# Keys and queries of the second linear attention computed with the tokens stationary, and turned by VectorE

## The reference, cut to what matters

```python
h = rms_norm_2(x, norm_mix_pre)
z = h @ w_in                                   # p, q, k, v, g_lr, r, gate_logits = split(z)
log_a = log_sigmoid(g_lr @ w_gate_up + b_gate) / 16
# 4 heads, keys of 256, values of 512, chunks of 64 tokens; per head:
qc = q * (256 ** -0.5); G = cumsum(log_a)      # within a chunk
A[i, j] = sum_c q[i, c] * k[j, c] * exp(G[i, c] - G[j, c])    # j <= i
o = A @ v + (q * exp(G)) @ S                   # S: state carried between chunks
```

## Time and profile before

| | |
|---|---|
| median of three runs | 2775.2 us (2774.86 to 2776.15) |
| the profiled execution | 2776.08 us |
| its span, first to last instruction | 2774.3 us |
| mean granted TensorE clock | 0.999 of full |
| PE busy | 2751.3 us (99%) |
| DVE busy | 1778.4 us (64%) |
| ACT busy | 1354.2 us (49%) |
| POOL busy | 64.8 us (2%) |
| share of PE in the chain that ended last | 96% |

### The profile page before, as it was taken

The page is one execution under the profiler, slowest core; times in us unless marked ns, Lnnn a source line. Parts: engine busy times, 40 slices in busy tenths (PEclk is TensorE's granted clock), DMA queues, the critical chain, the costliest instruction groups (busy, mean ns, idle before and its releaser), DMA issues.

```text
span 2774.3 us, 36245 instructions
## 1 busy us (share of the span) xinstructions
PE 2751.3 (99%) x14792; PEld 2302.3 (83%) x14792; DVE 1778.4 (64%) x2183; ACT 1354.2 (49%) x1635; POOL 64.8 (2%) x55
## 2 busy tenths in 40 slices
PE   9999999999999999999999999999999999999998
PEld 7888888878888888888888887888878888888887
DVE  6778865576556655766778744566566546656575
ACT  5666554654444434445546545554454444444443
POOL 0000000000000000000011000000000000000000
PEclk9999999999999999999999999999999999999999
DMA  8555455556656565555555554555555555565655
GB/s 325 188 167 171 157 186 167 185 180 205 195 191 190 198 196 192 194 187 176 192 171 171 176 194 163 179 201 195 196 190 183 204 194 191 191 198 188 198 190 159
DMA packets 144424, 525.16 MB, mean 189 GB/s; under 512 B 16081, under 2 KB 16641, under 8 KB 143617
## 3 DMA queue, kind: packets, MB, share of 16 engines
q1 hardware_dynamic: 142528, 514.71, 56.3%
q0 software_dynamic: 1440, 7.88, 0.8%
q10 hardware_dynamic: 288, 0.24, 0.0%
HBM read 520.66 MB, written 2.11 MB: 188 GB/s over the span
## 4 chain that ended last, share of the span: by engine, by line
PE 96%; DVE 2%; ACT 1%; issue 1%; DMA 0%; POOL 0%; DVEq 0%; SPq 0%; POOLq 0%; ACTq 0%
PE PS L539 96%; PE PS L542 0%; DVE X L1553 0%; DVE AR L1547 0%; DVE RL L1547 0%; DVE A_HL L1553 0%; ACT RH L1051 0%; DMA RAW<-in_stream 0%; DVE B_HL L1553 0%; ACT SP L1051 0%; POOL ST L2224 0%; ACT A_HL L1051 0%; ACT B_HL L1051 0%; DVE AR L1755 0%; DVE AR L1550 0%
## 5 line engine op out<-in xcount | busy, mean ns | idle before, releaser
L1547 DVE TENSOR_TENSOR RL<-RAW,RH 128x1024 fp32r<-128x1024 f32 x954 | 1159.3, 1225 | 863.2 <-ACT RH L1051 861.8
L1051 ACT ACTIVATE RH<-RAW 128x1024 fp32r<-128x1024 f32 (+1 forms) x962 | 1014.2, 1059 | 1049.2 <-PE PS L539 1032.9
L539 PE MATMUL PS<-RH,A_HL 128*128 128x512 f32 x3520 | 1094.5, 390 | 1.4 <-DVE A_HL L1553 0.9
L539 PEld LDWEIGHTS PS<-RH,A_HL 128*128 128x128 f32 x3520 | 660.7, 188 | 139.7 <-DVE A_HL L1553 1.1
L539 PE MATMUL PS<-RH,B_HL 128*128 128x512 f32 x2240 | 692.1, 389 | 2.1 <-DVE B_HL L1553 0.9
L539 PE MATMUL PS<-RL,A_HL 128*128 128x512 f32 x1760 | 684.8, 389 | 0.0
L539 PEld LDWEIGHTS PS<-RH,B_HL 128*128 128x128 f32 x2240 | 420.4, 188 | 90.5 <-DVE B_HL L1553 1.2
L539 PE MATMUL PS<-RL,B_HL 128*128 128x512 f32 x1120 | 435.7, 389 | 0.0
L539 PEld LDWEIGHTS PS<-RL,A_HL 128*128 128x128 f32 x1760 | 330.5, 188 | 68.7 <-issue 0.7
L539 PE MATMUL PS<-A_HL,RH 128*128 128x512 f32 (+1 forms) x1488 | 360.7, 394 | 4.2 <-DVE A_HL L1553 4.2
L539 PEld LDWEIGHTS PS<-A_HL,RH 128*128 128x128 f32 (+1 forms) x1488 | 271.1, 189 | 59.1 <-issue 3.5
(11 more groups left out here) (114 smaller groups left out, 961.4 us busy)
## 6 DMA issues: line engine op xcount, KB each, us to landing
RAW<-in_stream SPq DMA_DIRECT2D x959, 512.0 KB, 4.2
X<-in_x SPq DMA_DIRECT2D x4, 512.0 KB, 7.4
AR<-in_mem SPq DMA_DIRECT2D x4, 512.0 KB, 5.8
AR<-in_mem_turned SPq DMA_DIRECT2D x4, 512.0 KB, 5.6
out_x<-X SPq DMA_DIRECT2D x8, 256.0 KB, 2.8
AR<-in_x_turned SPq DMA_DIRECT2D x3, 512.0 KB, 8.2
AR<-scratch POOLq DMA_DIRECT2D x1, 1024.0 KB, 10.1
AR<-in_mix_post_g POOLq DMA_DIRECT2D x1, 1024.0 KB, 9.0
```

The source lines that it names most:

```text
L539: return g.matmul(o, l, r, start=start, stop=stop, skip_group_check=True)
L1051: return g.activation(o, i, f, bias=bias, scale=scale, accum_out=accum)
L1547: return g.tensor_tensor(o, a, b, f)
```

## The change

The four products K0, K1, Q0 and Q1 go from `by_feature` to `by_token`, and the stream holds their weights in blocks of 512 columns (as many slots as before). ACT alone evicts them, two activations of 128x512 for each, which scale by the token's row scale (for Q by a column `query_col`, row scale times 1/16, that ACT makes in `row_task`). DVE's additions and multiplications by RR fall away for them. They land in U(7) (two places, `KQ_ROWS`, used in turn), and a new task turns them to their old homes: 16 stream transposes of 32 partitions x 256 elements for each of the four, 64 in all, spread over the ticks last(name) + 0.5 to last(name) + 2. Both halves of the levels start 2.5 slots later, DECAY + 19.5 and DECAY + 27.5, and wait for the turned keys and queries (`s_kqt`).

```diff
-    by_columns("K0", "w_in_2", 16, 2048, 2)
+    by_tokens("K0", "w_in_2", 0, 16, 2048, 2)
     passes.append(("LR", "w_in_2", 0, 16, 5120, 16, 2))
-    by_columns("K1", "w_in_2", 16, 2048 + 512, 2)
+    by_tokens("K1", "w_in_2", 0, 16, 2048 + 512, 2)
     for j in range(2):
-        by_columns(f"Q{j}", "w_in_2", 16, 1024 + 512 * j, 2)
+        by_tokens(f"Q{j}", "w_in_2", 0, 16, 1024 + 512 * j, 2)
...
-            plan, at, done = level_plan([0, 1, 2, 4, 8, 16, 32, 64, 128], DECAY + (17, 25)[j], 8, 4, 1, hg_done[j], gla_at)
+            plan, at, done = level_plan([0, 1, 2, 4, 8, 16, 32, 64, 128], DECAY + (19.5, 27.5)[j], 8, 4, 1, hg_done[j], gla_at)
...
+        KQ_HOME = [U(1)[:, 0:1024], U(1)[:, 1024:2048], U(0)[:, 0:1024], U(0)[:, 1024:2048]]
+        KQ_ROWS = [U(7)[:, 1024 * k:1024 * k + 1024] for k in range(2)]
...
                         g.wait_ge(s_z_a, 8)
-                        g.wait_ge(s_free_v, read_v[f"Q{j}"])
+                        g.wait_ge(s_kqt, 3 + j)
...
-            by_feature("K0", A_HL, normed(3))
+            by_token("K0", AH, AL, normed(3))
...
-            for n in ("K1", "Q0", "Q1", "P0", "P1", "G00", "G01", "G02", "G03"):
+            for n in ("K1", "Q0", "Q1"):
+                by_token(n, AH, AL)
+            for n in ("P0", "P1", "G00", "G01", "G02", "G03"):
                 by_feature(n, A_HL)
...
+                if n == 3:
+                    act(query_col, row_col[n], scale=0.0625).then_inc(s_rw, 1)
...
+            def keyed(n):
+                def evict(banks):
+                    g.wait_ge(s_rrs, 4)
+                    if n > 1:
+                        g.wait_ge(s_kqt, n - 1)
+                    for b in range(2):
+                        t = act(KQ_ROWS[n % 2][:, 512 * b:512 * b + 512], PS[:, banks[b], :],
+                                scale=(row_col[3], query_col)[n // 2][:, b:b + 1])
+                    t.then_inc(s_free_a, 1)
+                return evict
...
+            def keys_turn_task():
+                for n, name in enumerate(KQ):
+                    src = KQ_ROWS[n % 2].rearrange("p (b c d i) -> p b c d i", b=2, c=4, d=4)
+                    dst = KQ_HOME[n].rearrange("p (c b d i) -> p b c d i", c=4, b=2, d=4)
+                    for fq in range(4):
+                        yield last(name) + 0.5 + 0.5 * fq
+                        g.wait_ge(s_free_a, read_a[name])
+                        for tq in range(4):
+                            t = g.transpose(dst[32 * fq:32 * fq + 32, :, :, tq, :], src[32 * tq:32 * tq + 32, :, :, fq, :])
+                    t.then_inc(s_kqt, 1)
...
             def gla_inputs(j):
-                return [(s_z_v, 11 + 3 * j), (s_free_v, read_v[f"Q{j}"])]
+                return [(s_z_v, 11 + 3 * j), (s_kqt, 3 + j)]
...
-            through("K0", rowed(U(1)[:, 0:1024], 3))
+            through("K0")
...
-            through("K1", rowed(U(1)[:, 1024:2048], 3))
+            through("K1")
             for j in range(2):
-                through(f"Q{j}", rowed(U(0)[:, 1024 * j:1024 * j + 1024], 3, 0.0625))
+                through(f"Q{j}")
```

More of the change, by code:

```diff
@@ L318, in build @@
         s_vh, s_va = sem("first_values_multiplied"), sem("first_values_copied")
+        s_kqt = sem("second_keys_turned")
         s_c_m, s_c_a, s_c_v = sem("cross_by_tensor"), sem("cross_by_scalar"), sem("cross_by_vector")
@@ L343, in build @@
         ffn_readers("F")
-        by_vector += ["K0", "LR", "K1", "Q0", "Q1", "P0", "P1"] + [f"{n}{j}" for n in ("G0", "ya") for j in range(4)]
+        by_scalar += ["K0", "K1", "Q0", "Q1"]
+        by_vector += ["LR", "P0", "P1"] + [f"{n}{j}" for n in ("G0", "ya") for j in range(4)]
         by_scalar += [f"{n}{j}" for n in "VR" for j in range(4)]
@@ L406, in build @@
         GLA_END = last("V0")
+        KQ = ["K0", "K1", "Q0", "Q1"]
         def hg_at(t):
@@ L511, in build @@
         row_col = [stat(f"row_scale{n}", 2) for n in range(5)]
+        query_col = stat("query_scale", 2)
         neglam, lb, oml, subg = stat("neglam", 1), stat("lb", 8), stat("oml", 8), stat("subg", 1)
@@ L707, in row_task @@
                 g.wait_ge(s_nlo, 8 * n + 8)
-                g.wait_ge(s_rw, SPREAD[n])
+                g.wait_ge(s_rw, SPREAD[n] + (n == 3))
                 w = SP4[:, 0:T].rearrange("p (b n) -> p b n", b=2)
@@ L1474, in scalar @@
             norm(3, AH, last("Fo2_3") + 1)
-            through("K0", None, U(1)[:, 0:1024])
+            def keyed(n):
[8 more added lines that the diff above has]
+                return evict
+            through("K0", keyed(0))
             def low_rank(banks):
@@ L1480, in scalar @@
             through("LR", low_rank)
-            through("K1", None, U(1)[:, 1024:2048])
+            through("K1", keyed(1))
             for j in range(2):
-                through(f"Q{j}", None, U(0)[:, 1024 * j:1024 * j + 1024])
+                through(f"Q{j}", keyed(2 + j))
             for j in range(2):
@@ L1980, in vector @@
                           *[level_task(j, gla_plan[j], gla_homes(j), 2, [6 + j], gla_inputs(j), 2) for j in range(2)],
-                          pool_task(), gla_out_task(), row_task(4), hidden_task(0), hidden_task(1))
+                          keys_turn_task(), pool_task(), gla_out_task(), row_task(4), hidden_task(0), hidden_task(1))
             def post_part(n, b, ssq):
```

## The result

The changed kernel takes **2788.1 us** (median of 4 runs, 2787.57 to 2789.92), the kernel before 2775.4 (4 runs, 2774.86 to 2776.15): 1.0045 times as long, 95% interval 1.0033 to 1.0057. The forecast was 2776.6, which is 11.5 us less, and its range ended at 2779.5.

A forecast was written before the change was run, and what follows sets the result against it. The prediction took TensorE's pace to bound the kernel (busy 99% of the span). Pace -1.5, entry into K0 +1.4 and the wait behind Q0 +1.5 summed to +1.4 us, from 2775.2 to 2776.6 us, range 2774.0 to 2779.5.

The forecast's parts named there:

- The levels' move: Levels 2.5 slots later, takes now between two evictions: longest stretch without a low half shorter; cost 0, bounds 0 and 1.2.
- The burst behind K1: VectorE's transposes begin 3.5 us after K1's end (F); slot 462's low half in time by 0.4 us, cost nothing.
- The burst behind Q0: VectorE's transposes end 13.8 us after Q0's end (E); TensorE waits 1.5 us at level 0 in slot 469.
- The entry into K0: K0 ends at 1316.9 in place of 1315.5, its third slot waiting for a low half: cost 1.4 us, bounds 0.7 and 2.0.
- the forecast wait for the third slot: In K0, TensorE reaches the third slot at about 1298.8 and waits for VectorE's low half, starting at 1300.2.
- The pace: Slots by token take 2.721 us, by feature 2.784; 24 slots of K1, Q0 and Q1 gain 1.5 us, bounds 0 and 2.0.
- The single-matmul rule: N/2.4 + 2.5 ns per matmul: a token slot 2.590 us, a feature slot 2.600, gain 0.24 us for 24 slots.
- The chances: Whole kernel: 0.02 for faster by over 0.2%, 0.91 for within 0.2%, 0.07 for slower by over 0.2%.
- rival (d): VectorE's queue so full that each of four bursts makes a low half 1.2 us late: 2781.5 us, chance 0.07.
- the signs that were to show the forecast wrong: TensorE idle behind K0, K1 or Q1 bursts, slot pace not 2.72, or K0 ending under 0.7 or over 2 us later.
- those that were to show it right: Among them: K0's third-slot wait, a 1.5 us wait in Q1, no TensorE idle P0 to V0, VectorE over 90% busy LR to P0.

The follow-up runs named there:

- e1: Kernel before with only the two level plans moved to DECAY+19.5 and DECAY+27.5, no transposes: 2783.3 us, ratio 1.0027.
- e2: Changed kernel with the levels another 1.5 slots later, at DECAY+21 and DECAY+29: 2781.4 us, ratio 1.0019.
- e5: Changed kernel with one take and its spans, of both halves, moved from between slots 502 and 503 to behind slot 504: 2782.3 us, ratio 1.0022.
- e3: Changed kernel with the first of the decay's two exponentials on ScalarE 1.5 slots later, DECAY+8.5 instead of DECAY+7: 2784.8 us, ratio 1.0031.
- second profile: Changed kernel unchanged, profiled again in the second set of runs: span 2786.1 us; that set's median 2787.5 us, ratio 1.0041.
- e7: Changed kernel with e3's edit, levels at +21 and +29, slot 488's take at 489.5, high part first in all but each product's last slot: 2775.5 us, ratio 0.9999.
- e10: Changed kernel with e9's levels, e3's edit, and high part first in all slots of K0, K1, Q0, Q1 but each one's last: 2776.6 us, ratio 1.0003.
- e4: Changed kernel with K0's first three slots multiplying the high part first, waiting for the low part only in between: 2785.6 us, ratio 1.0035.
- e6: Changed kernel with the levels back at DECAY+17 and DECAY+25, so the transposes' part alone: 2797.0 us, ratio 1.0077.
- e9: Changed kernel with levels back at +17 and +25, except each half's first: products at DECAY+21 and +29, take and spans at +21.5 and +29.5: 2780.8 us, ratio 1.0016.

## Why the prediction was wrong

- **The levels' move, costed at 0 with bounds 0 and 1.2: this step failed, by 7.4 us** (e1). It reasoned that takes between two evictions make the longest stretch without a low half shorter, and looked for their effect on low halves and on V0's eviction. The low halves were fine. Who waited was ScalarE, for an eviction behind the takes, and then the pool through ScalarE. I had listed VectorE's fullest place (1430 to 1475) and not the stage behind it. There VectorE and ScalarE have idle time (9.4 and 15.0 of the 45 us from 1475 to 1520 in the kernel before), but the chain of dependences goes through three engines. e2, with the levels later still, shows that lateness as such does not cost this, and e5 that the place of the takes at one tick does. No rival had this mechanism.
- **The burst behind K1, costed at 0: wrong by 1.9 us of wait.** With what follows the wait, Q0 lost 2.2 us in the first profile and 3.9 in the second, where the clock fell (+1.73 and +3.35, and 0.5 of gained pace on top). The time from the burst's begin to its end was right: 1352.32 to 1360.76 are 8.4 us, and the low half of slot 462 ended 9.7 us behind the begin, as worked out. The begin was not: F + 6.0 (F = 1346.35) in place of F + 3.5. The model is from a place without decay activations, and ScalarE was passed with "idle half of the time". A share over the kernel says nothing of the two instructions that stand at one tick (e3). The margin was 0.4 us, so any such row decided.
- **The burst behind Q0, +1.5: right in the first profile** (1.54 us of idle time before level 0, its transposes over at E + 13.8 as worked out, E = 1370.36). There TensorE and VectorE both came over 2 us late out of the burst behind K1, which the working did not have. But e3, whose burst behind K1 begins at F + 3.6 as forecast, has 1.41, so this is not luck. The second profile has 0.58 there, since TensorE came about 1 us later, behind a longer Q0. Waits in a row are not independent: what is lost at one is partly given back at the next.
- **The entry into K0, +1.4: right**, +1.3 to +1.7 in the seven traces with the order of the changed kernel. The first profile hid the forecast wait for the third slot: the first slot ran in part at the lower clock (0.92 in the mean from 1295 to 1320) and took 4.7 us. e3 and e5 show the wait itself, 1.15 and 1.19 us, and the same end.
- **The pace, -1.5: right.** K1 takes 23.22 us in place of 23.71, -0.49, in all ten traces with K1 by token, and where no wait disturbs (e7, e10) K1, Q0 and Q1 gain 1.5 together. The single-matmul rule of the Trainium skill ("TensorE: Matmul & The Clock Gate", Back-to-back issue gap) would leave an estimated 0.24 us of the 1.5. The traces do not agree with it: K1 alone gains 0.49.
- **The chances.** 0.91 for within 0.2% and 0.07 for slower rested on rival (d), a full VectorE at four bursts, and it wasn't the cause: the largest loss needs no transpose (e1), one burst of four made a low half late, and that one through ScalarE (e3). The bounds "0 to 1.2" for each unknown edit were bounds for one low half, not for an instruction that others wait for.

Of the signs that were to show the forecast wrong, one came, idle time behind the K1 burst. Of those that were to show it right, two did not come besides the hidden wait in K0: TensorE had idle time between P0 and V0, and VectorE was busy for 59.4 of 69 us from LR on (86%) and not for over 90%.

By term for the second profile: entry +1.3 (forecast +1.4), pace -1.5 in K1 to Q1 (-1.5), slot 462 with the clock behind it +3.9 (0), level 0 +0.7 (+1.5), pool +6.1 (0), slots 525 and 473 to 504 +1.1 (0). Sum +11.6.

## What to carry to other kernels

An edit that only moves ticks has to be costed at every tick on which it lands: for each, list what stands behind the moved instruction in its engine's order, and who waits for those, to the second and third engine, also far behind the code that was edited. Where a burst has under 1 us of margin, read the rows of all engines at that very tick, since an idle share over the kernel hides a table load and an exponential. When a late operand meets an engine with independent work in the same slot, the order within the slot can cover it: in e4 it took K0 with its entry from +1.3 us to -0.3.

## What the runs showed of the hardware

The same idle time of TensorE was sometimes followed by a lower granted clock and sometimes not. Busy time in the 10 us around the wait at slot 462, for the first profile (us; PE, PEld, DVE, ACT and POOL busy; granted clock, DMA share, GB/s):

```profile
1360.00:1370.00 10.00, 8.14 (x36) 6.59 (x36) 9.92 (x11) 3.18 (x3) 0.00 (x0) 1.00 0.61 209
```

and for the second profile, the same columns:

```profile
1358.00:1368.00 10.00, 8.14 (x29) 6.41 (x29) 9.92 (x10) 2.60 (x3) 0.00 (x0) 0.83 0.60 205
```

TensorE was idle 1.85 and 1.86 us and busy alike. In the second the granted clock fell to 1.2 GHz behind the wait (0.83 in the mean), which cost 1.6 us (Q0 +3.35 in place of +1.73). Of the seven profiles with this wait, four have the lower clock (the second profile, e5, e6 and e9) and Q0 at +3.3 to +3.4, and three have 1.00 and Q0 at +1.7 to +1.8. Behind the 4.2 us of idle time at the pool the granted clock fell in all five profiles in which the wait stands, 0.77 to 0.89 in the mean over 15 us (1495 to 1510), and the wait of 4.2 cost 6.0 to 7.1 us. In e6 waits of 7.4 and 6.4 us cost 9.9 and 8.3. So behind these waits 1.8 to 3.0 us were lost beyond the wait itself wherever the clock fell, for 1.9 us and for 7.4 us alike, and 0.4 where it did not (with the 0.5 us of pace added that Q0 and Q1 otherwise gain). Here it was a sum that came on top, not a share of the wait. What decides in the case of 1.9 us stays open.
